# Expert rows gathered as quarters and turned by VectorE, w1 and w3 loaded in 4 KB pieces

## What is computed

```python
def _hier_moe(h, wg, bg, we, be, w1, w3, w2):
    lg = (hf @ wg + bg); g_idx = argmax(lg)                # 4 groups
    le = (hf @ we + be).reshape(n_tok, 4, 8)[g_idx]        # 8 experts of the group
    top_p, top_i = lax.top_k(softmax(le), 2)
    ...
    # assignments sorted by expert, padded to blocks of 128 slots
    a = jax.nn.silu(xblk @ w1[e]) * (xblk @ w3[e])         # 1024 -> 512
    return a @ w2[e]                                       # 512 -> 1024
    ...
    y = zeros.at[sorted_tok].add(yb[dest] * sorted_gate)
```

## Time and profile before

| | |
|---|---|
| median of 3 runs | 2226.88 us (2222.35 to 2228.76) |
| the profiled execution | 2228.8 us, its span 2226.9 us |
| TensorE busy | 2033.2 us (91%) |
| VectorE busy | 1215.5 us (55%) |
| ScalarE busy | 1116.0 us (50%) |
| GpSimd busy | 363.2 us (16%) |
| DMA | 476.90 MB, mean 214 GB/s |

### The profile page before, as it was taken

The page is one execution under the profiler, slowest core; times in us unless marked ns, Lnnn a source line. Parts: engine busy times, 40 slices in busy tenths (PEclk is TensorE's granted clock), DMA queues, the critical chain, the costliest instruction groups (busy, mean ns, idle before and its releaser), DMA issues. The chain is left out here.

```text
span 2226.9 us, 30743 instructions
## 1 busy us (share of the span) xinstructions
PE 2033.2 (91%) x9213; PEld 1436.8 (65%) x9214; DVE 1215.5 (55%) x1115; ACT 1116.0 (50%) x1323; POOL 363.2 (16%) x325
## 2 busy tenths in 40 slices
PE   3999999999999977979999399999999999999990
PEld 2436778777666322337777388888787788888870
DVE  6653223234667744834444753656778666565644
ACT  6871222226566322523333255657778666565634
POOL 0690000000000320310000021222121122121220
PEclk9998999999999999979999699999999999999995
DMA  6691222321234987966433476888999988886848
GB/s 217 240 326 36 76 67 76 95 76 40 52 76 148 347 309 308 351 213 220 158 131 104 151 248 205 266 286 283 376 306 378 319 287 273 288 282 202 291 139 320
DMA packets 240654, 476.90 MB, mean 214 GB/s; under 512 B 25121, under 2 KB 87717, under 8 KB 235431
## 3 DMA queue, kind: packets, MB, share of 16 engines
q1 hardware_dynamic: 201800, 383.62, 47.8%
q0 software_dynamic: 15424, 58.78, 11.0%
q10 hardware_dynamic: 23360, 33.56, 4.7%
HBM read 355.24 MB, written 114.29 MB: 211 GB/s over the span
## 5 line engine op out<-in xcount | busy, mean ns | idle before, releaser
L1860 PE MATMUL p<-wh_hi,x_hi 128*128 128x512 f32 x768 | 308.0, 401 | 1.7 <-DVE x_lo L1974 0.6
L1860 PE MATMUL p<-wh_hi,x_lo 128*128 128x512 f32 x768 | 303.8, 396 | 0.0
L1860 PE MATMUL p<-wh_lo,x_hi 128*128 128x512 f32 x768 | 303.4, 395 | 0.0
L1986 DVE TENSOR_TENSOR wh_lo<-w_raw,wh_hi 128x2048 fp32r<-128x2048 f32 x128 | 284.8, 2286 | 27.5 <-ACT wh_hi L1947 27.5
L540 PE MATMUL ps<-h_hi,wp_hi 128*128 128x512 f32 x640 | 257.4, 402 | 4.3 <-DVE wp_lo L735 4.3
L540 PE MATMUL ps<-h_lo,wp_hi 128*128 128x512 f32 x640 | 254.1, 397 | 0.0
L540 PE MATMUL ps<-h_hi,wp_lo 128*128 128x512 f32 x640 | 254.0, 397 | 0.0
L1947 ACT ACTIVATE wh_hi<-w_raw 128x2048 fp32r<-128x2048 f32 x128 | 234.8, 1924 | 0.2 <-DMA w_raw<-in_exp_w_dram 0.2
L1860 PEld LDWEIGHTS p<-wh_hi,x_hi 128*128 128x128 f32 x768 | 144.4, 188 | 36.1 <-issue 1.7
L1860 PEld LDWEIGHTS p<-wh_hi,x_lo 128*128 128x128 f32 x768 | 144.2, 188 | 35.5
L1860 PEld LDWEIGHTS p<-wh_lo,x_hi 128*128 128x128 f32 x768 | 144.6, 188 | 33.5
(11 more groups left out here) (321 smaller groups left out, 3463.9 us busy)
## 6 DMA issues: line engine op xcount, KB each, us to landing
w_raw<-in_exp_w_dram SPq DMA_DIRECT2D x512, 256.0 KB, 5.9
w_raw<-in_exp_w_dram SPq DMA_DIRECT2D x128, 512.0 KB, 10.9
dec<-in_decay_dram SPq DMA_DIRECT2D x32, 512.0 KB, 5.7
scratch_KA<-work SPq DMA_DIRECT2D x32, 512.0 KB, 4.6
scratch_SI<-arena SPq DMA_DIRECT2D x32, 512.0 KB, 4.3
kin<-scratch_KA SPq DMA_DIRECT2D x21, 512.0 KB, 7.4
arena<-scratch_SA SPq DMA_DIRECT2D x21, 512.0 KB, 6.2
wp_raw<-in_w_in_dram SPq DMA_DIRECT2D x18, 512.0 KB, 3.7
```

The source lines that it names most:

```text
L1860: mm = pe.matmul(acc[:, :], x[:, k, :], w, start=(k == 0 and i == 0), stop=(k == n - 1 and i == 2))
L1986: dve.tensor_tensor(lo, raw[:, j:j + 2, :], hi.bitcast(F32), ALU.subtract).then_inc(lowered, 1)
```

## The change

H2 is written with its columns in another order. Column d = 256 q + 8 a + k of the normed row is stored as quarter q, then k, then a; ScalarE copies `h` into that order (`h_quarters`) before the transfer. The routing makes four index columns for each block instead of one: four small matmuls pick, for partition 32 q + b and j, the token of slot 32 j + b, times 4, and `quarter` adds q. Four indirect transfers then gather 128 quarters of 1 KB each into `xg[:, j]`. One VectorE transpose of 128 x 1024, which turns each 32 x 32 square by itself, leaves in `xT` the 128 channels 8 p + k of all 128 slots on partition p. TensorE's transposes of x are gone, and `x_hi` and `x_lo` are made from `xT` in SBUF, with views that put j and b side by side. Since the channel of partition p and chunk k is now 8 p + k, w1 and w3 are loaded with the same order: two rows of 2 KB that lie side by side in DRAM are one piece of 4 KB.

```diff
@@ output_projection, ScalarE
-                act.dma_start(dram["H2"][t * P:t * P + P, :], h[:, t % 2, :]).then_inc(h_out[t % 2], 16)
+                at_least(act, h_out, 16 * t)
+                act.activation(h_quarters[:, :, :, :], h[:, t % 2, :].rearrange("p (q a k) -> p q k a", q=4, k=KC), ACT.Copy).then_inc(quartered, 1)
+                act.wait_ge(quartered, t + 1)
+                act.dma_start(dram["H2"][t * P:t * P + P, :], h_quarters.rearrange("p q k a -> p (q k a)")).then_inc(h_out, 16)
@@ route, TensorE
             last.then_inc(idx_mm, 1)
+            pe.wait_ge(token_ready, BASE + 1)
+            for j in range(4):
+                last = pe.matmul(pq[:, j * IDX_COLS:(j + 1) * IDX_COLS], pick[:, j, :, :].rearrange("p q b -> p (q b)"), token[:, :], start=True, stop=True)
+            last.then_inc(picked, 1)
@@ route, VectorE
+            step(dve.tensor_scalar(pick[:, :, :, :], by_quarter, 4.0, None, ALU.mult))
...
-            step(dve.tensor_scalar(idx[:, :], pr[:, 0:IDX_COLS], 1.0, 1.0, ALU.max, ALU.subtract))
+            dve.tensor_scalar(token[:, :], pr[:, 0:IDX_COLS], 1.0, 1.0, ALU.max, ALU.subtract).then_inc(token_ready, 1)
...
+            dve.wait_ge(picked, BASE + 1)
+            dve.tensor_scalar(idx.rearrange("p j n -> p (j n)"), pq[:, 0:4 * IDX_COLS], quarter[:, 0:1], None, ALU.add).then_inc(idx_set, 1)
@@ experts, SP
-                        src = dram[name].rearrange("o e (k p) f -> p (o e) k f", p=P)[:, ds(e, 1), k]
+                        for c, name in enumerate(("exp_w1", "exp_w3")):
+                            src = dram[name].rearrange("o e (p k) f -> p (o e) k f", p=P)[:, ds(e, 1), j:j + 2]
+                            sp.dma_start(slabs[:, pair, c], src.rearrange("p a k f -> p (a k) f")).then_inc(raw_in[pair], 16)
@@ experts, GpSimd
-                pool.indirect_dma_start(out=xg[:, :], out_offset=None, in_=dram["H2"],
-                                        in_offset=bass.IndirectOffsetOnAxis(ap=cur[:, :], axis=0)).then_inc(xg_in, 16)
+                for j in range(4):
+                    pool.indirect_dma_start(out=xg[:, j, :], out_offset=None, in_=quarter_rows,
+                                            in_offset=bass.IndirectOffsetOnAxis(ap=cur[:, j:j + 1], axis=0)).then_inc(xg_in, 16)
...
-                pool.wait_ge(trx, BASE + B * 2 + 2)
-                pool.wait_ge(xg_in, B * 16 + 16)
+                pool.wait_ge(trx, BASE + B + 1)
+                pool.wait_ge(xg_in, B * 64 + 64)
@@ experts, TensorE
-            transpose_x(0)
...
-                transpose_x(B + 1)
@@ experts, ScalarE
+                act.wait_ge(trx, BASE + B + 1)
...
-                    act.activation(x_hi[:, 4 * h:4 * h + 4, :], px[h].rearrange("p (k n) -> p k n", k=4), ACT.Copy).then_inc(xhi_ready, 1)
+                    act.activation(by_j(x_hi[:, some, :]), x_turned[:, some], ACT.Copy).then_inc(xhi_ready, 1)
@@ experts, VectorE
+            def turn(B):
+                dve.wait_ge(xg_in, B * 64 + 64)
+                dve.wait_ge(xhi_ready, BASE + B * 2)
+                dve.wait_ge(xlo_ready, BASE + B * 2)
+                dve.transpose(xT[:, :], xg.rearrange("p j d -> p (j d)")).then_inc(trx, 1)
+                dve.wait_ge(trx, BASE + B + 1)
...
                 split_a(B)
+                turn(B + 1)
```

More of the change, by code:

```diff
@@ L1239, in output_projection @@
         rw_zero, both_ready = sem("rw_zero", 0), sem("both_ready", 0)
-        h_out, x2_out = [sem(f"h_out{s}", 0) for s in range(2)], [sem(f"x2_out{q}", 0) for q in range(4)]
+        h_out, quartered, x2_out = sem("h_out", 0), sem("quartered", 0), [sem(f"x2_out{q}", 0) for q in range(4)]
         LG, tables, next_phase = yield sem
@@ L1480, in _ @@
             copy_logits(NT // 2 - 1)
-            for s in range(2):
-                act.wait_ge(h_out[s], 16 * (NT // 2))
+            act.wait_ge(h_out, 16 * NT)
             for q in range(4):
@@ L1580, in put @@
             return nc.alloc_sbuf_tensor_at(name, shape, dt, offset=offset)
-        tri, ones, pos8, thr, tok, line, again, pad = (tables[n] for n in ("tri", "ones", "pos8", "thr", "tok", "line", "again", "pad"))
+        tri, ones, pos8, thr, tok, line, again, pad, quarter = (tables[n] for n in ("tri", "ones", "pos8", "thr", "tok", "line", "again", "pad", "quarter"))
         hit16, row16, col16 = (put("wy", n, [P, 2, NT, width], F16) for n, width in (("hit16", IDX_COLS), ("row16", P), ("col16", IDX_COLS)))
@@ L1586, in route @@
         sb = lambda name, shape, dt=F32: put("xg", name, shape, dt)
-        blank = sb("blank", [P, IDX_COLS])
+        blank, token, pick = sb("blank", [P, IDX_COLS]), sb("token", [P, IDX_COLS], F16), sb("pick", [P, 4, 4, P // 4], F16)
         place_i, place = sb("place_i", [P, 2, 2, NT], I32), sb("place", [P, 2, 2, NT])
@@ L1739, in experts @@
         PAIRS, H_PAIRS = SLABS // 2, KC // 2
-        raw_in = [sem(f"raw_in{r}") for r in range(SLABS)]
+        raw_in = [sem(f"raw_in{r}") for r in range(PAIRS)]
         pool_passed, act_passed = sem("pool_passed"), sem("act_passed")
@@ L1861, in products @@
                 return mm
-            def transpose_x(B):
-                pe.wait_ge(xg_in, B * 16 + 16)
-                for h in range(2):
-                    pe.wait_ge(xlo_ready, BASE + B * 2 + h - 1)
-                    for k in range(4 * h, 4 * h + 4):
-                        last = pe.transpose(px[h][:, (k % 4) * P:(k % 4 + 1) * P], xg[:, k * P:(k + 1) * P], ident[:, :])
-                    last.then_inc(trx, 1)
             def transpose_a():
@@ L1984, in split_w @@
                     dve.wait_ge(rounded, BASE + e * PAIRS + pair + 1)
[L1985 to L1986 removed]
+                    if pair < H_PAIRS:
+                        dve.tensor_tensor(by_part(wh[1], j), slabs[:, pair], by_part(wh[0], j).bitcast(F32), ALU.subtract).then_inc(lowered, 1)
+                    else:
+                        hi, lo = (v[:, r * FT + j - KC:r * FT + j - KC + 2, :] for v in wy)
+                        dve.tensor_tensor(lo, raw[:, j:j + 2, :], hi.bitcast(F32), ALU.subtract).then_inc(lowered, 1)
             dve.memset(py[0][:, :], 0.0)
@@ L1991, in _ @@
             split_w(0, 0, 0, range(2))
+            turn(0)
             split_x(0)
@@ L2126, in build @@
         next(output, None)
-        expert.send((nblk, idx, spot, weight))
+        expert.send((nblk, idx, spot, weight, xT))
         routing.send((LG, weight, idx, spot, nblk, tables))
```

75 lines of the change are left out of this document (43 added, 32 removed).

## The result

The changed kernel takes 2235.49 us (median of 11 runs, 2230.75 to 2240.95), the kernel before 2226.17 (11 runs, 2222.35 to 2230.78). The ratio is 1.0042, 95% interval 1.0031 to 1.0054: 9.3 us slower. The forecast was 2202.

The account below looks back on a forecast made before the run. Bound by TensorE at 18.12 us a block and, in ten experts, DMA at 19.60 us each. -41.8 + 3 + 8.5 + 5.2 = -25.1, against the median 2202 us; range 2190 to 2226.

Parts of the forecast that it names:

- TensorE: Expert stage: eight transposes leave each block's chain, 18.12 to 17.25 us, -41.8 us over 48 blocks.
- 3.6 us of cover: Output stage: next tile's `z` is done at 1157.80, TensorE takes it at 1161.42, hiding ScalarE's 1.1 us copy.
- what would make me wrong altogether: Output stage: the closing sign, that ScalarE's copy delays this stage; no size or chance given.
- It is now 0.10 late, 0.15 with a semaphore: Expert changes: down products wait for `a_lo`; 21 changes at 0.15 us give +3 us.
- VectorE becomes the bound: Rival, 12 in 100: the turn takes 2.3 us, `x_lo` is 0.8 late at lone one-block experts; +5, 2207 us.
- just hidden, with 0.2 us left: Expert changes: after a 1.29 us turn, `x_lo` ends at +20.5, before the next `wh_lo` pair's due time, +20.70.
- The DMA's pace: Runs of one-block experts: 19.6 to 19.4 us an expert; losses 15.3 instead of 6.75, +8.5 us.
- Before the first block: Start: products 6.2 us later, `pick` and late H2 store 0.6 each, first block 11.20 not 13.42; +5.2 us.
- The gathers come late: Rival, 18 in 100: between close expert changes, gathers held by `wh_lo` delay VectorE's turn; +16, 2218 us, at the top 2232.
- the packets of 1 KB are dear: Rival, 10 in 100: each costs 142 ns like a 4 KB packet, DMA pace 22.5; +44, 2246 us.

Follow-up runs that it names:

- the pairs: Changed kernel with w1 and w3 split so only two neighbouring channels share a partition, the quarter copy reading every second element: 2221.81 us, ratio to before 0.9983.
- the run with another order: Changed kernel with VectorE, ahead of the first block, told to await the gathers' issue, then split one weight pair instead of two: 2232.68 us, ratio to before 1.0030.

## Why the prediction was wrong, point by point

**TensorE: right.** 18.12 us became 17.24 to 17.25 wherever no expert changes.

**The step that failed first: "ScalarE's copy to `h_quarters` is a 128x1024 pass, 1.06 us ... 3.6 us cover 1.1 sixteen times; without cover it would be 17."** The price failed: the copy took 2.23 us because of its step of 32 bytes; the contiguous one took 1.06. Forecast 0; taking the copy out gave 16.1 us.

And by 3.6 us of cover even 2.23 would have been hidden, so the cover was wrong as well. It was read at the transposes of `z`, but TensorE needs VectorE's chain earlier, for its `small` products (the code lets them wait for the `ms` that `st<-small` sets). Before:

```profile
1156.74 0.15 DVE L1520 TENSOR_SCALAR st<-small 128x1 f32<-128x1 f32 x1
...
1159.54 1.95 PE L1378 MATMUL small<-hT,rw 128*64 128x256 f32 x16
```

That leaves 2.65 us. The changed copy put the square 2.72 us later behind `hT` (4.11 against 1.39: the copy and 0.5 us of waits), the contiguous one 1.58 and the pairs 1.73 (each read at one tile). The last two are under the 2.65, and they cost nothing in the twelve inner tiles; the first is over it, and TensorE stopped at `small`. So the conclusion "covered" was right for a copy of 1.06 us in the inner tiles, and wrong for the copy that was made, and for the first two tiles and the last.

I had named the copy as what would make me wrong altogether, and yet gave it no rival and no part of the range, though no row of before shows its access pattern.

**"It is now 0.10 late, 0.15 with a semaphore": the lateness was right, its price wasn't.** `a_lo` was 0.18 us late. TensorE then lost 0.95 us: 0.18, 0.52 to go on, 0.25 in the down products. The stop cost five times the lateness. From 1311.78 to the end of the last products at 2167.51 the chain took 855.7 us; 47 x 17.24 and 11.20 are 821.5, the first block has 2.4 more, and 31.8 us are left over for 31 expert changes. 16 of them stand behind experts of two blocks, at 0.95 to 0.97 each, about 15.4 in all: this is `a_lo`, where the forecast had 3, and putting it first gave back 12.8. The other 15 stand behind experts of one block, at 0.84 (18.08 less 17.24), 12.6 in all: they are the next point. Together 28.

**The rival "VectorE becomes the bound" came true, for another reason and at more than twice its price (12.6 us, not 5).** The turn took 1.26 us, not 2.3. I had `x_lo` end at +20.5 and the next `wh_lo` due at +20.70, "just hidden, with 0.2 us left". But the next `wh_lo` isn't due at a fixed time behind the products: between the turn and it stand ScalarE's `x_hi` and first `wh_hi`, which leave VectorE idle for 0.90 us in the earlier trace rows and for 0.95 to 1.03 now, and I left them out of the loop. It closes at 18.08, not at 17.25, in the changed kernel and in the run with `a_lo` first. Working this rival out with the turn's length alone is what hid it.

**The DMA's pace: the size was too dear.** Measured is 19.07 us an expert in the second of the runs, from one load of w2 to the next but one, two experts on:

```profile
1718.91 14.36 DMA w_raw<-in_exp_w_dram
...
1757.05 14.16 DMA w_raw<-in_exp_w_dram
```

Forecast 19.4, before 19.60. The runs lost about 4 us by the DMA (31.8 less 28), forecast 15.3, before 6.75: most of what the DMA owed was already lost in VectorE's loop of 18.08 us. So the experts' sum is -41.8 + 28 - 3 + 0 = -17, measured -16.1, forecast -32.5.

**Before the first block: the mechanism right, the size small.** The +7.4 ahead of the first product (6.2 + 0.6 + 0.6) were +12.7 (2.9 + 9.8, the third and fourth lines of the table), 1.8 of them the copy of the last tile. The held gather took 3.47 us, the landing 7.04 instead of 4.1. And the first block gave back nothing where 2.2 us were forecast: these belonged to the granted clock (0.84 before, 0.83 after), not to weights.

**The gathers come late, and the packets of 1 KB are dear: wrong.** With one gather in place of four the experts took 927.2 us, as with four.

## What to carry to other kernels

- Work that is moved to change a layout has a price of its own, by its access pattern: look for a row with the same step in bytes, and where there is none, let the range hold twice the contiguous price. Then ask what stands behind it on its engine; behind the instruction that others wait for, the same 2.3 us cost nothing between the squares. And read the cover at the first thing that the bound engine needs from the chain (here 2.6 us), not at a later one (3.6), and at the first and last tiles too.
- When a bound engine gets faster by 0.87 us, engines that finished just in time can be late next. Go round the whole loop of each, waits for other engines included. Here a new stop of TensorE cost 0.8 us on top of 0.18 us of lateness.
- Two edits that both pay (fewer TensorE cycles, larger DMA pieces) can be hidden by a third that only makes them possible. Run each alone.

## What the runs showed of the hardware

- Reading 128x1024 fp32 at a step of 32 bytes took 2.23 us on ScalarE and 2.32 on GpSimd; contiguous it took 1.06 on ScalarE. VectorE needed 0.77 us for 256 columns with two sources at that step, against 1.28 for 1024 contiguous ones: four such instructions take 2.4 times as long.
- One VectorE transpose of 128x1024 fp32 (32 x 32 squares) took 1.23 to 1.25 us.
- TensorE, stopped for 0.18 us by a late operand, lost 0.95 us in all.
- GpSimd's semaphore increment behind four gathers in program order had taken effect at the latest 0.4 us into the second.
- One gather's issue took 3.47 us beside VectorE's `wh_lo`, an instruction with two SBUF sources, where the other three of the same start took 0.94 to 1.18 (the run with another order).
